# Gate and up products of a feed-forward stage: one 512-column product for both parts of the activations, and a VectorE sum behind the root

## The reference

```
h = rms_norm(x, ffn_norm)                       # 256 x 1024
f = (silu(h @ w_gate) * (h @ w_up)) @ w_down    # width 2816 in between
x = x + f                                       # layer 0: x + rms_norm(f)
```

## Time and profile before

| | us |
|---|---|
| median of three runs | 1064.37 |
| the profiled execution, its own time | 1054.86 |
| its span, first to last instruction | 1053.1 |
| PE busy | 1020.2 (97%) |
| DVE busy | 683.4 (65%) |
| ACT busy | 502.8 (48%) |
| mean granted TensorE clock | 0.991 |

### The profile page before, as it was taken

The page is one execution under the profiler, slowest core; times in us unless marked ns, Lnnn a source line. Parts: engine busy times, 40 slices in busy tenths (PEclk is TensorE's granted clock), DMA queues, the critical chain, the costliest instruction groups (busy, mean ns, idle before and its releaser), DMA issues. The chain is left out here.

```text
span 1053.1 us, 20188 instructions
## 1 busy us (share of the span) xinstructions
PE 1020.2 (97%) x8778; PEld 964.2 (92%) x8778; DVE 683.4 (65%) x1080; ACT 502.8 (48%) x663; POOL 4.8 (0%) x9
## 2 busy tenths in 40 slices
PE   8999889999999999999999999999999999999996
PEld 7898789999998988869999999999886899999996
DVE  5867476776555887745665555587866476555554
ACT  5466554344444663443643434465535465344442
POOL 1000000000000000000000000000000000000000
PEclk9999999999999999999999999999999999999999
DMA  8535235555554232212554545543231155454531
GB/s 306 185 104 186 101 105 194 196 193 198 169 198 155 81 122 90 82 41 102 195 188 175 197 168 193 183 148 107 92 118 43 41 200 192 169 201 162 198 121 41
DMA packets 23736, 156.41 MB, mean 149 GB/s; under 512 B 2576, under 2 KB 3776, under 8 KB 6112
## 3 DMA queue, kind: packets, MB, share of 16 engines
q1 hardware_dynamic: 21600, 151.70, 40.0%
q10 hardware_dynamic: 1840, 2.50, 0.7%
q0 software_dynamic: 208, 0.92, 0.3%
HBM read 154.05 MB, written 1.06 MB: 147 GB/s over the span
## 5 line engine op out<-in xcount | busy, mean ns | idle before, releaser
L445 PE MATMUL bank<-h_hi,w_hi 128*128 128x256 f32 x1480 | 426.1, 288 | 10.4 <-DVE h_lo L1539 4.6
L1532 DVE TENSOR_TENSOR w_lo<-raw,w_hi 128x2048 fp32r<-128x2048 f32 (+3 forms) x144 | 323.4, 2250 | 162.2 <-ACT w_hi L1107 161.6
L445 PE MATMUL bank<-h_lo,w_hi 128*128 128x256 f32 x1480 | 420.3, 284 | 0.0
L445 PE MATMUL bank<-h_hi,w_lo 128*128 128x256 f32 x1480 | 420.2, 284 | 0.0
L1107 ACT ACTIVATE w_hi<-raw 128x2048 fp32r<-128x2048 f32 (+3 forms) x144 | 269.2, 1873 | 87.5 <-PE bank L445 82.4
L445 PEld LDWEIGHTS bank<-h_hi,w_hi 128*128 128x128 f32 x1480 | 285.1, 193 | 17.8 <-issue 8.3
L445 PEld LDWEIGHTS bank<-h_lo,w_hi 128*128 128x128 f32 x1480 | 285.2, 193 | 1.0 <-issue 0.7
L445 PEld LDWEIGHTS bank<-h_hi,w_lo 128*128 128x128 f32 x1480 | 285.2, 193 | 0.0
L445 PE MATMUL bank<-mix_hi,w_hi 128*128 128x256 f32 x720 | 205.5, 285 | 1.9 <-DVE mix_lo L1514 1.4
L445 PE MATMUL bank<-mix_hi,w_lo 128*128 128x256 f32 x720 | 203.8, 283 | 0.0
L445 PE MATMUL bank<-mix_lo,w_hi 128*128 128x256 f32 x720 | 203.8, 283 | 0.0
(11 more groups left out here) (308 smaller groups left out, 882.4 us busy)
## 6 DMA issues: line engine op xcount, KB each, us to landing
raw<-in_w SPq DMA_DIRECT2D x136, 1024.0 KB, 4.8
raw<-in_w SPq DMA_DIRECT2D x5, 512.0 KB, 3.9
raw<-in_w SPq DMA_DIRECT2D x2, 896.0 KB, 4.4
raw<-in_w SPq DMA_DIRECT2D x2, 768.0 KB, 4.3
cst<-in_consts SPq DMA_DIRECT2D x1, 1314.0 KB, 12.4
x<-in_x SPq DMA_DIRECT2D x2, 512.0 KB, 6.8
arena<-bias_rows ACTq DMA_DIRECT2D x1, 1024.0 KB, 6.0
out<-arena ACTq DMA_DIRECT2D x4, 256.0 KB, 2.0
```

Of the source, the lines that this page charges most:

```text
L445: last = pe.matmul(dst, w[a](k), act[b](k), start=start and i == 0 and j == 0, stop=stop and i == n - 1 and j == 2, skip_group_check=loose)
L1532: dve.tensor_tensor(w_lo[:, s, 0:n], raw[:, s, 0:n], w_hi[:, s, 0:n].bitcast(F32), ALU.subtract)\
```

## The change

`h_hi` and `h_lo` become the two halves of one tile `h_both`, at the same place. `wide_product` replaces `product` for gate and up: for each k-tile one matmul of `w_hi` against both halves (512 columns, filling a bank: `w_hi*h_hi` in its first half, `w_hi*h_lo` in its second), then `w_lo*h_hi` of 256 columns into the first half. Gate and up of a block so take two banks; blocks alternate between banks 4 and 5 and banks 6 and 7, and `gate_up(j)` waits for `gu` of block j-2. The sum of squares of this stage goes to bank 0, which is free by then. `feed(j)` now multiplies each of the two banks by `rstd` into a new tile `both`, and adds the halves into `gu`.

```diff
+        h_both = sb("h_both", [P, 2, KT, T], F32R)
+        h_hi, h_lo = h_both[:, 0, :, :], h_both[:, 1, :, :]
...
-        def gate_up_bank(j):
-            return pairs((4, 5, 7)[j % 3])
+        def gate_up_bank(j, t):
+            return pairs(4 + 2 * (j % 2) + t)
...
+            def wide_product(dst, w, k_tiles, start=True, stop=True):
+                for k in k_tiles:
+                    pe.matmul(dst, w[0](k), h_both[:, :, k, :], start=start and k == 0, stop=False, skip_group_check=True)
+                    last = pe.matmul(dst[:, 0, :], w[1](k), h_hi[:, k, :], start=False,
+                                     stop=stop and k == KT - 1, skip_group_check=True)
+                return last
...
-                    if j >= 3:
-                        pe.wait_ge(V.sem, V.at(l, "gu", j - 3))
+                    if j >= 2:
+                        pe.wait_ge(V.sem, V.at(l, "gu", j - 2))
...
-                            last = product(gate_up_bank(j)[:, t, :], tile_of(c, KT, 2 * P, t * P), range(KT), H)
+                            last = wide_product(gate_up_bank(j, t), tile_of(c, KT, 2 * P, t * P), range(KT))
...
-                inverse_root(rstd[:, :], bank[6][:, 0:T], 1.0 / D, Mc("eps"), (l, what, "rstd"))
+                inverse_root(rstd[:, :], bank[0 if what == "ffn" else 6][:, 0:T], 1.0 / D, Mc("eps"), (l, what, "rstd"))
...
-                    tt(FF["gu"][:, j % 2, :, :], gate_up_bank(j), wide(rstd[:, :], 2), ALU.mult, l, "gu", j)
+                    for t in range(2):
+                        last = tt(FF["both"][:, t, :, :], gate_up_bank(j, t), wide(rstd[:, :], 2), ALU.mult)
+                    last.then_inc(V.sem, V.mark(l, "gu_both", j))
+                    after_v(l, "gu_both", j)
+                    tt(FF["gu"][:, j % 2, :, :], FF["both"][:, :, 0, :], FF["both"][:, :, 1, :], ALU.add, l, "gu", j)
```

More of the change, by code:

```diff
@@ L237, in program @@
         h_at = nc.sbuf_base
-        h_hi, h_lo = sb("h_hi", [P, KT, T], F32R), sb("h_lo", [P, KT, T], F32R)
+        h_both = sb("h_both", [P, 2, KT, T], F32R)
+        h_hi, h_lo = h_both[:, 0, :, :], h_both[:, 1, :, :]
         mix_hi, mix_lo = sb("mix_hi", [P, KT, T], F32R), sb("mix_lo", [P, KT, T], F32R)
@@ L288, in program @@
         xg, sq = NORM["xg"], NORM["sq"]
-        FF, _ = area(0, dict(gu=(2, 2, T), sg=(2, T), act=(2, T)))
+        FF, _ = area(0, dict(gu=(2, 2, T), sg=(2, T), act=(2, T), both=(2, 2, T)))
         act_hi, act_lo = mix_hi[:, 0:4, :], mix_lo[:, 0:4, :]
@@ L468, in norm_sum @@
                 if what in ("in", "ffn"):
+                    into = 6 if what == "in" else 0
                     pe.wait_ge(V.sem, V.at(l, what, "sum", 2))
@@ L495, in as_they_come @@
                                         split(pe, c)
+                                    if what == "ffn":
+                                        wide_product(b(t), tile_of(c, KT, width, at), (k,), stop=False)
+                                        continue
                                     product(b[:, t, :], tile_of(c, KT, width, at), (k,), H,
@@ L506, in as_they_come @@
                                 split(pe, c)
+                            if what == "ffn":
+                                last = wide_product(b(t), tile_of(c, KT, width, at), (2 * m, 2 * m + 1))
+                                continue
                             last = product(b[:, t, :], tile_of(c, KT, width, at), (2 * m, 2 * m + 1), H,
@@ L649, in ffn @@
                 c = CHUNK[l, "gu", 0]
-                pieces = [(1, gate_up_bank(0), [(c, 2 * P, 0), (c, 2 * P, P)]),
-                          (0, gate_up_bank(1), [(c + 1, 2 * P, 0)])]
+                pieces = [(1, lambda t: gate_up_bank(0, t), [(c, 2 * P, 0), (c, 2 * P, P)]),
+                          (0, lambda t: gate_up_bank(1, t), [(c + 1, 2 * P, 0)])]
                 as_they_come(l, "ffn", pieces[:2 if l == 0 else 1])
```

## The result

The changed kernel takes 1095.35 us (median of four executions, 1093.32 to 1115.23) against 1065.36 for the kernel before (four executions, 1064.28 to 1070.32). The ratio is 1.033, 95% interval 1.026 to 1.040, which is clearly slower; the two medians alone stand at 1.028. The medians are 30 us apart, where +34.3 was forecast. The profiled execution is a typical one: its own time is 1095.16, its span 1093.3.

What follows compares the result with a forecast made beforehand. PE, busy 97% of the span, was taken to bound the kernel, with DVE's round close behind. 19.6 + 4.0 + 6.1 + 2.4 + 7.5 - 5.3 = 34.3 us on 1064.4 gave 1098.7 us, range 1083 to 1112.

Steps and rivals of the forecast that it cites:

- new wait at block 2: Each layer's block 2: PE stands still 6.54 us until gu of block 0 comes; 19.6 us over three layers.
- clock behind it: Behind each block 2 gap: a half-clock stretch costing 2.5 us, three times, 7.5 us; ends 0 and 10.2.
- odd blocks of layer 0: Four layer 0 pairs with rope angles: DVE late by 7.4 us, less 3.4 in hand; 4.0 us of stall.
- last `down`, layers 0, 1, 2: Stage ends: PE waits for act_lo before the second half, 4.7, 1.4 and 0 us; sum 6.1.
- seams: Between layers: DVE begins its first sum into x later, so each seam grows 1.2 us, twice; 2.4.
- products: Gate and up k-tiles: 355 ns in place of 360, over 1056 k-tiles; a gain of 5.3 us.
- Rival (d): Block 2: the new wait isn't felt, gu of block 0 comes in time; 1071.6 us, chance 0.01.
- just hidden: Ordinary feed-forward pairs: the longer feed makes DVE's round 17.14 us against PE's 17.12, so no stall there.
- (b): Gate and up: the wide product costs 260 ns, its operand lying in two places; k-tile 380 ns, 1115 us, chance 0.10.
- (c): Not slower: weight load, not columns, sets the 120 ns; k-tile 320 ns, 1049 us if stalls stay hidden, chance 0.03.
- The offset: Whole kernel: the shown median lies 9.5 us above the profiled execution, 1054.86, and this difference was taken as fixed.
- Rival (a): Only block 2's new wait counts; the clock holds, angles and ends stay hidden; 1078.7 us, chance 0.15.

Runs made afterwards that it cites:

- e5: Changed kernel with 13 float32 matmuls into a free bank ahead of block 2's wait, to keep PE busy; 1090.34 us, ratio 1.0242 to the kernel before.
- e1: Kernel before with the new wait alone: gate_up(j) waits for gu of block j-2 in place of j-3; 1087.08 us, ratio 1.0225.
- e6: Changed kernel where ACT copies second halves out, DVE adds them ahead of the root, and PE waits for that sum; 1071.75 us, ratio 1.0104.
- e8: e6 with block 0's copy and sum ahead of chunk 3's rounding and split, and layer 1's last split behind the first sum into x; 1069.11 us.
- e4: Changed kernel with block 2 in banks 2 and 3, free until the first down; 1105.42 us, ratio 1.04 to the kernel before.
- e3: Changed kernel with the short feed: only the gate's bank is multiplied, halves not added; 1083.23 us, ratio 1.0191 to the kernel before.
- e9: Kernel before, unchanged, profiled a third time; 1064.35 us.
- e2: Kernel before with the longer feed alone: same bank multiplied twice and halves added, products and waits as before; 1084.41 us, ratio 1.0233.

## Why the prediction was right, and where it was not

Profiled execution against profiled execution the change costs 1095.16 - 1054.86 = 40.3 us. By the steps of the prediction:

| step | forecast | measured |
|---|---|---|
| new wait at block 2 | 19.6 | 6.76 + 6.63 + 6.63 = 20.0 |
| clock behind it | 7.5 | 1.41 + 1.63 + 1.65 = 4.7 (by e5 1.8 and 1.7 in layers 1 and 2) |
| odd blocks of layer 0 | 4.0 | 5.7 |
| last `down`, layers 0, 1, 2 | 4.7, 1.4, 0 | 4.4, 2.5, 0 |
| clock in the last `down`, layers 0, 1 | none | 2.3 + 1.6 = 3.9 |
| pauses under 0.2 each, layer 0 | none | 0.6 |
| seams | 2.4 | -0.6 and -0.4, counted in the next line |
| mixers, start and tail | 0 | 5.7, of which layer 2's mixer 4.0 |
| products | -5.3 | -7.4 |
| sum | 34.3 | 40.1 (the profiles differ by 40.3) |

(A gap counts without the 0.12 us that lie between two starts anyway. The clock's lines are what the matmuls of a half-clock stretch take above their pace at the full clock. The products' line is for the 984 k-tiles within the stages' bounds.)

**The new wait: right, and shown.** 6.54 forecast, 6.63 in layers 1 and 2. e1 brings the gap alone, less the longer feed (5.43). With PE's order unchanged, e6 leaves 1.2 to 1.5 of it by making the awaited step a short one, and e8 takes the rest away by bringing that step forward. Rival (d) is out. That it is DVE's order and not the number of banks is what e4 showed, against my own theory at that point.

**The longer feed: right in place, small in size.** Layer 0's odd blocks were forecast at 4.0, between blocks 7 and 15, and came to 1.32 + 2.09 + 1.77 + 0.97 - 0.48 = 5.7, from start to start. The first three, at blocks 9, 11 and 13, make 4.8. The fourth is at block 17, outside the forecast's blocks. By the rows it comes from a term that the forecast did not have: four operations of ACT for the rope angles stand ahead of the rounding that DVE's split waits for:

```profile
280.51 1.32 ACT L1244 ACTIVATE rope<-rope 128x256 f32<-128x256 f32 x4
283.67 2.29 DVE L1551 TENSOR_TENSOR w_lo<-raw,w_hi 128x2048 fp32r<-128x2048 f32 x1 [0.74 <-ACT w_hi L1126]
```

The end of layer 1 was forecast at 1.4 and came to 2.5. One of the odd blocks on PE, and the middle of layer 1's last `down`, the answers to the earlier trace rows:

```profile
241.67 0.47 PE L456 MATMUL bank<-h_both,w_hi 128*128 128x512 f32 x1 [1.81 <-DVE arena L1533]
...
716.58 0.28 PE L448 MATMUL bank<-mix_hi,w_lo 128*128 128x256 f32 x1
719.17 0.54 PE L448 MATMUL bank<-mix_hi,w_hi 128*128 128x256 f32 x1 [2.31 <-DVE mix_lo L1533]
719.50 0.42 PE L448 MATMUL bank<-mix_lo,w_hi 128*128 128x256 f32 x1
```

I had called ordinary pairs "just hidden", DVE's round 17.14 against PE's 17.12. In the trace DVE's splits come back after 17.16:

```profile
575.77 2.29 DVE L1551 TENSOR_TENSOR w_lo<-raw,w_hi 128x2048 fp32r<-128x2048 f32 x1 [1.38 <-ACT w_hi L1126]
...
592.93 2.29 DVE L1551 TENSOR_TENSOR w_lo<-raw,w_hi 128x2048 fp32r<-128x2048 f32 x1 [1.38 <-ACT w_hi L1126]
```

and PE's pair with the cheaper product takes 32 x 0.353 + 48 x 0.120 = 17.06. In layer 1 its `down` chunks do start 17.07 apart, nine times in a row, while DVE's splits keep to 17.16. So DVE falls 0.1 us further behind in each pair, and nine or ten pairs make most of the 1.1 that the end of layer 1 has more (this last is worked out, not tried). Of the 2.45 us that PE gains on the way in layer 1 a good part is thus waited for at the end.

**The products: right, small in size.** 353 ns, not 355: the narrow matmul behind a wide one takes 117. (The prediction says "nearly the same number of columns"; it is the same number, 512 + 256 for 3 x 256.) Rivals (b) and (c) are out; e3 and layer 2 of e8 show 2.45 us per stage. The Trainium skill (TensorE: Matmul & The Clock Gate, Back-to-back issue gap) gives an estimated 216 and 109 by its formula for isolated matmuls, and 131 as a sustained figure for 512 columns. The measured 236 and 117 agree with neither, and no dense stretch of 512-column products in any run here came near 131.

**The clock: right at block 2, missed elsewhere.** The fall came with each of the three gaps and cost 1.4 to 1.6 us each, where 2.5 was taken (in e1 and e3 1.8 to 2.4). What failed is that I looked for it only there. The last `down` of layers 0 and 1 runs all or most of its second half at 0.50 too, 5.08 and 4.36 us from its first start to its last in place of 2.76 (3.9 in all). That also is why the seams did not grow: PE reached the end late, DVE was ready, and the gap to layer 2 went from 2.19 to 1.80. In e4, where the clock held in layer 1's last `down`, that seam did grow, by 1.1. The mixers had 10.2 us stretches where there were 6.8 and none.

**The offset: wrong.** The step "I take the difference as fixed" failed. It was no property of the measurement: a typical execution of before holds some 24 us more at half clock than the profiled one, in a mixer, which the change does not touch, and pays 10 for it (e9). The changed kernel's profile has 10.2 us there and not 30.7, so the offset did not carry over. Two errors, 9.5 too much offset and some 6 us too little for everything else, cancel in part; 1098.7 against 1095.35 is closer than the working deserved. Taken against typical executions the change costs 30 us; the three stages alone are 34.5 longer, and the mixers give the rest back in the comparison.

Rival (a), that only the wait counts, is refuted by e2: the feed alone makes the kernel 2.3% slower.

**What stays open.** Which executions get the long stretch in a mixer, and why a kernel with shorter feed-forward stages (e8) gets more of it, I can't say. By the listed clocks e8's executions have 34 to 64 us at half clock, 55 in the mean, those of before that ran beside them 32. By before's line these 23 us are worth some 9.5, about the difference of the medians (8.8). e8's own seven executions lie on 1045.3 + 0.407 x that time. So at equal time at half clock e8 is only about 1 us ahead of before, where its expectation had an intercept of 1040 to 1043; and none of its longer executions was profiled. Nor is it shown why layer 2's mixer got a stretch of 10.2 us at half clock in the changed kernel.

## What to carry to other kernels

Fewer and wider matmuls over the same columns save little, here 7.5 ns in 360; before taking them, count what the other engines must do more per block, and lay their round beside PE's, since a round 0.1 us longer is a debt that the end of the stage pays. A new wait is priced by what stands ahead of the awaited step in the other engine's order, and here moving that step forward took the gap away, where other banks only moved it (e8 and e4); neither made the kernel faster than before. Where single executions of one kernel differ by more than their interval, list the mean clock of each before any difference is called an effect or an offset, and compare profiles stage by stage.

## What the runs showed of the hardware

- The operand of a matmul may be two runs of 256 columns from different places at no price: 236 ns for 512 columns, against 235 for one run.
- Every idle time of PE of 3.6 to 6.6 us in the stages of any run came with a fall to half clock. Of those near 2 us some did and some did not: 1.91 (block 11 in e4 and in e5), 2.06 (the end of layer 0 in e6 and e8), 2.22 (e5) and 2.31 (the changed kernel, both at the end of layer 1) did; 1.81 (block 11, the changed kernel), 1.92, 2.03 (e3, the seam to layer 2) and 2.10 (e4, end of layer 1) did not. So the length of a gap alone does not tell. 13 float32 matmuls of no use ahead of the wait held the clock (e5).
- The half clock with such a gap costs 1.2 to 2.6 us and is over after 3.4 or 6.8. In a mixer it can last 30.7 to 34.1 us with PE busy throughout, and layer 1's mixer is then 10 to 12 us longer. The same program has it in some executions and not in others.
